# Expert stage of a 256-token transformer kernel: exact one-hot scatter into X, a moved branch, a reordered router

## The reference

```
logits = t @ w_router                                  # t: 256 x 1024, w_router: 1024 x 8
top_vals, top_idx = lax.top_k(logits, 2)
top_w = softmax(top_vals)
gates = sum(one_hot(top_idx, 8) * top_w)               # 256 x 8, two entries a row
for e in range(8):
    out = out + gates[:, e] * (silu(t @ w_gate[e]) * (t @ w_up[e])) @ w_down[e]
x = x + g2 * out                                       # g2: one row of 1024 of the modulation
return rmsnorm(x, final_norm)                          # then the second block
```

## Time and profile before

| | us |
|---|---|
| three runs | 2864.95, 2864.95, 2858.27 (median 2864.95) |
| the profiled execution | 2863.4 |
| its span from first to last instruction | 2861.5 |

### The profile page before, as it was taken

One profiled execution on the slowest core, in us unless ns is written; L12 is line 12 of the kernel. 1 busy time (PEld: TensorE's weight loads), 2 busy tenths in 40 slices (PEclk: granted clock), 3 DMA queues, 4 the chain that ended last, 5 costly groups with the idle time before them and its releaser, 6 DMA issues.

```text
span 2861.5 us, 38958 instructions
## 1 busy us (share of the span) xinstructions
PE 2668.1 (93%) x15384; PEld 2311.5 (81%) x15384; DVE 1982.5 (69%) x2853; ACT 1550.9 (54%) x2238; POOL 29.1 (1%) x40
## 2 busy tenths in 40 slices
PE   7688998978999999999996998998999999998998
PEld 3677988856888888888885997887898998787898
DVE  4768878886798899889896556555555556555555
ACT  2443444553777778777774444464444444364444
POOL 0000000020000000000000000000000000000000
PEclk9789998989999999999998999999999999999999
DMA  8537974614799999999995664433565664433563
GB/s 279 188 96 283 343 273 123 193 40 130 274 368 341 335 355 355 332 336 368 339 356 167 190 187 154 126 96 111 178 184 167 193 183 145 155 96 110 162 185 118
DMA packets 349599, 616.34 MB, mean 215 GB/s; under 512 B 20705, under 2 KB 174881, under 8 KB 349409
## 3 DMA queue, kind: packets, MB, share of 16 engines
q1 hardware_dynamic: 346402, 603.35, 63.1%
q0 software_dynamic: 1872, 5.99, 0.7%
q10 hardware_dynamic: 1136, 4.44, 0.4%
HBM read 612.66 MB, written 1.05 MB: 214 GB/s over the span
## 4 chain that ended last, share of the span: by engine, by line
PE 80%; DVE 11%; ACT 5%; DMA 2%; issue 2%; SPq 0%; DVEq 0%; ACTq 0%
PE pb L286 23%; PE pb L288 23%; PE pb L287 23%; PE pb L292 8%; DVE parts L260 3%; PE pb L408 2%; ACT parts L245 2%; DVE mod L1657 1%; DMA raw<-in_w_in 1%; PE pb L2609 1%; PE pb L2154 1%; DVE raw L625 1%; DMA raw<-in_ffn_w_up 0%; DMA X<-in_x 0%; DVE hTl L421 0%
## 5 line engine op out<-in xcount | busy, mean ns | idle before, releaser
L260 DVE TENSOR_TENSOR parts<-raw,parts 128x1024 fp32r<-128x1024 f32 (+2 forms) x1051 | 1263.7, 1216 | 614.9 <-ACT parts L245 580.4
L245 ACT ACTIVATE parts<-raw 128x1024 fp32r<-128x1024 f32 (+2 forms) x1051 | 1101.6, 1054 | 832.4 <-PE pb L288 693.9
L286 PE MATMUL pb<-parts,arenar 128*128 128x512 f32 (+2 forms) x1696 | 667.1, 393 | 12.6 <-DVE arenar L421 6.0
L287 PE MATMUL pb<-parts,arenar 128*128 128x512 f32 (+2 forms) x1696 | 649.9, 383 | 0.0
L288 PE MATMUL pb<-parts,arenar 128*128 128x512 f32 (+2 forms) x1696 | 649.5, 383 | 0.0
L286 PE MATMUL pb<-hTh,parts 128*128 128x256 f32 x1952 | 558.2, 286 | 6.0 <-DVE hTl L421 3.5
L287 PE MATMUL pb<-hTl,parts 128*128 128x256 f32 x1952 | 557.0, 285 | 0.0
L288 PE MATMUL pb<-hTh,parts 128*128 128x256 f32 x1952 | 556.8, 285 | 0.0
L286 PEld LDWEIGHTS pb<-hTh,parts 128*128 128x128 f32 x1952 | 379.7, 195 | 9.8 <-issue 5.2
L286 PEld LDWEIGHTS pb<-parts,arenar 128*128 128x128 f32 x1696 | 321.7, 190 | 76.9 <-issue 16.4
L287 PEld LDWEIGHTS pb<-hTl,parts 128*128 128x128 f32 x1952 | 379.7, 195 | 1.8
(11 more groups left out here) (286 smaller groups left out, 1996.5 us busy)
## 6 DMA issues: line engine op xcount, KB each, us to landing
raw<-in_moe_w_gate SPq DMA_DIRECT2D x176, 512.0 KB, 5.2
raw<-in_moe_w_up SPq DMA_DIRECT2D x176, 512.0 KB, 5.2
raw<-in_moe_w_down SPq DMA_DIRECT2D x176, 512.0 KB, 5.2
raw<-in_ffn_wg SPq DMA_DIRECT2D x88, 512.0 KB, 4.1
raw<-in_ffn_wu SPq DMA_DIRECT2D x88, 512.0 KB, 3.8
raw<-in_ffn_wd SPq DMA_DIRECT2D x88, 512.0 KB, 4.4
raw<-in_ada_wT SPq DMA_DIRECT2D x80, 512.0 KB, 5.2
raw<-in_w_in SPq DMA_DIRECT2D x72, 512.0 KB, 3.7
```

Source lines behind the costliest of these rows:

```text
L245: a.e.activation(self.part(t, 0), self.slot(t), ACT.Copy).then_inc(*a.up(self.c.hi, t.m))
L260: v.e.tensor_tensor(self.part(t, 1), self.slot(t), self.part(t, 0).bitcast(F32), ALU.subtract).then_inc(*v.up(self.c.lo, t.m))
L286: e.matmul(o, a[0], b[0], start=start, stop=False, skip_group_check=True)
L287: e.matmul(o, a[0], b[1], start=False, stop=False, skip_group_check=True)
```

## The change

- `Pm` is turned itself (not `Pm` times the gate) and stored for single-pass matmuls, which are exact for zeros and ones. The gate of each place is formed as a column `gcol` by two more matmuls of one column in `gates_pe`.
- The result of an expert is scaled by `gcol` and by the row of the modulation on DVE, straight from PSUM (`result_dve`, two instructions of 512 columns). ACT makes its high part `yh` (`result_act`), DVE its low part `yl` (`result_parts_dve`), and each scatter is two single-pass matmuls. Its result is added straight to X. `acc`, its memset and `add_dve` are gone.
- The scatters stand after tiles 2, 4, 6 of step (e+1, 2) and tile 0 of step (e+1, 3); gathers and gates of the next expert move by a tile or two. Expert 7's scatters use four banks.
- The flag is loaded at step 6 of the loop; the branch stands before expert 7's result and scatters.
- The router forms the logits token-major, per half of the tokens, without copy and transposes, PE's part for the first half standing ahead of the transposes of the second. The modulation's row is formed after the counting. An Exp is run early, so that its table is loaded. Expert 0's second gather has a bank of its own.

```diff
+    def result_dve(self, v, e):
+        K, c = self.K, self.c
+        v.wait_ge(*c.pe.val(("down", e)))
+        v.wait_ge(*c.bk[4].out.val(("PmT", e)))
+        if e:
+            v.wait_ge(*c.dv.val(("yl", e - 1, 1)))
+        for h in range(2):
+            b, cs = self.y_bank(h), slice(h * 512, (h + 1) * 512)
+            v.e.scalar_tensor_tensor(out=self.y[:, cs], in0=b.t[:, :], scalar=self.gcol[:, e % 2:e % 2 + 1],
+                                     in1=K.mod[:, 2, cs], op0=ALU.mult, op1=ALU.mult).then_inc(*v.up(b.out, ("y", e, h)))
+    def result_act(self, a, e):
...
+        for h in range(2):
+            cs = slice(h * 512, (h + 1) * 512)
+            a.wait_ge(*self.y_bank(h).out.val(("y", e, h)))
+            a.e.activation(self.ysb[0][:, cs], self.y[:, cs], ACT.Copy).then_inc(*a.up(c.ac, ("yh", e, h)))
+    def result_parts_dve(self, v, e):
...
+            v.wait_ge(*c.ac.val(("yh", e, h)))
+            v.e.tensor_tensor(self.ysb[1][:, cs], self.y[:, cs], self.ysb[0][:, cs].bitcast(F32),
+                              ALU.subtract).then_inc(*v.up(c.dv, ("yl", e, h)))
     def scatter_pe(self, t, e, tt, h):
-        c, b = self.c, self.c.bk[7]
-        t.wait_ge(*c.bk[6].out.val(("y", e, 1)))
-        t.wait_ge(*c.bk[5].out.val(("y", e, 0)))
...
-        mm1(t.e, b.t[:, :], self.PgT[:, e % 2, tt * P:(tt + 1) * P],
-            self.ysb[:, h * 512:(h + 1) * 512]).then_inc(*t.up(c.pe, ("scatter", e, tt, h)))
+        t.wait_ge(*c.dv.val(("yl", e, h)))
...
+        for i in range(2):
+            m = mm1(t.e, b.t[:, :], self.PmT[:, e % 2, tt * P:(tt + 1) * P],
+                    self.ysb[i][:, h * 512:(h + 1) * 512], i == 0, i == 1)
+    SCATTER = [(2, 2), (2, 4), (2, 6), (3, 0)]
+    GATHER = [(3, 2), (3, 4)]
+    GATES = (3, 6)
     def gates_pe(self, t, e):
...
+        for tt in range(2):
+            m = mm1(t.e, b.t[:, S:S + 1], self.Pm[:, e % 2, tt, :], gate[:, tt * 8 + e:tt * 8 + e + 1], tt == 0, tt == 1)
     def up_dve(self, v, i):
...
             self.step_dve(v)
+            if e and (j, q) == (2, 0):
+                self.result_parts_dve(v, e - 1)
     def pe(self, t):
-        self.K.enter_pe(t, "m2")
+        self.K.stats_pe("m2")
+        for tt in range(2):
+            self.K.xT_pe(t, "m2", tt)
+            self.logits_pe(t, tt)
         self.router_pe(t)
-        self.main.pe(t)
-        self.more(t, self.extra.pe)
+        self.main.pe(t, self.keep)
+        self.more(t, self.flags[t], self.extra_pe)
+        self.main.end_pe(t)
```

More of the change, by code:

```diff
@@ L559, in enter_act, with enter_dve @@
         self.W.hi(a, 2)
-    def enter_dve(self, v, st, add, norm, by_rows=False):
+    def enter_dve(self, v, st, add, norm, by_rows=False, early=1):
+        early = 0 if by_rows else early
         add(v, 0)
@@ L567, in enter_dve @@
         self.xT_dve(v, st, 0, 0)
-        if not by_rows:
-            self.W.low(v)
+        self.W.low(v, early)
         norm(v, 1)
@@ L572, in enter_dve @@
             self.xT_dve(v, st, tt, h)
-        self.W.low(v, 4 if by_rows else 3)
+        self.W.low(v, 4 - early)
     def hT_lhs(self, k, tt):
@@ L2091, in up_pe @@
             b = c.bk[self.up_bank(i, w)]
-            t.wait_ge(*c.bk[7].out.val(("gather", e, 4)))
+            for g0 in (0, 4):
+                if g0 < k0 + kg:
+                    t.wait_ge(*c.bk[self.gather_bank(e, g0)].out.val(("gather", e, g0)))
             if k0 == 0:
@@ L2191, in down_act, with pe @@
             self.step_act(a)
-        if j < 5:
-            return
-        a.wait_ge(*c.pe.val(("down", e)))
-        if e:
-            a.wait_ge(*c.pe.val(("scatter", e - 1, 1, 1)))
-        for h in range(2):
-            b = c.bk[5 + h]
-            a.e.activation(self.ysb[:, h * 512:(h + 1) * 512], b.t[:, :], ACT.Copy).then_inc(*a.up(b.out, ("y", e, h)))
+        if j == 5 and e < 7:
+            self.result_act(a, e)
     def down_dve(self, v, i):
-        for f in range(GROUPS[self.steps[i][1]][1] // P):
+        e, j = self.steps[i]
+        for f in range(GROUPS[j][1] // P):
             self.step_dve(v)
-    def pe(self, t):
+        if j == 5 and e < 7:
+            self.result_dve(v, e)
+    def pe(self, t, meanwhile=lambda t: None):
         n = len(self.steps)
@@ L2292, in router_pe @@
         mm1(t.e, b.t[:, 16:24], K.C["ones"], mask[:, 8:16], False, True).then_inc(*t.up(c.pe, "places"))
+        K.rows_pe(t, 1, 1, 2, (2, 3))
     def router_act(self, a):
         K, c = self.K, self.K.c
-        b = c.bk[0]
-        a.wait_ge(*c.pe.val("logits"))
-        a.e.activation(self.lgT, b.t[0:8, 0:S], ACT.Copy).then_inc(*a.up(b.out, "logits"))
+        a.wait_ge(*a.tail)
+        a.e.activation(K.warm, K.warm, ACT.Exp).then_inc(*a.up(c.ac))
+        a.wait_ge(*c.dv.val("top_gap"))
+        w1 = two(self.w12)[:, :, 1:2]
+        a.e.activation(w1, w1, ACT.Exp).then_inc(*a.up(c.ac, "top_exp"))
         for h in range(2):
@@ L3234, in mid_dve @@
     def mid_dve(self, v):
-        for tt in range(2):
-            self.moe.add_dve(v, tt)
         for tt in range(2):
```

201 lines of the change are left out of this document (116 added, 85 removed).

## The result

The changed kernel takes **2887.51 us** (four runs, 2886.51 to 2888.35), the kernel before 2863.40 (four, 2858.27 to 2864.95): ratio 1.0087, 95% interval 1.0070 to 1.0105. It is slower, as forecast, and inside the range, but 24 us slower where the sum said 15. The profiled execution spans 2885.9 us against 2861.5, 24.4 more.

What follows compares the result with a forecast made beforehand. PE (TensorE) was taken to bound the expert loop, DVE and ACT chains the stretches outside it. Seams +27.7, flag +1.0, end -11.4 and entry -2.6 gave +14.7 on 2863.4, so 2878 us; range 2860 to 2895.

Steps and rivals of the forecast that it cites:

- Scatter: Expert loop: single-pass scatters save 0.42 to 0.43 us each, four an expert, 1.7 us for each of seven experts.
- Chain: Each seam between experts: PE waits for `yl` at the first scatter, 3.5 us lost, bounds 3.0 and 4.3.
- Clock: After each seam's wait: PE drops to 1.2 GHz for eight matmuls, 1.6 us lost a seam, lower bound 0.
- low end of 2869: Whole kernel: the forecast time in us with all bounds low; all high gave 2897.
- Gates: Expert loop: two float32 matmuls of one column cost 0.45 us an expert, bounds 0.2 and 0.7.
- Seam: Each of seven seams between experts: net loss of 3.95 us from scatter, gates, waits and clock, 27.7 us in all.
- Flag: Mid-loop load of the flag on PE: costs 1.0 us, between 0 and 2.8.
- End: After the last down matmul: the norm starts earlier, gain 11.4 us, bound 6; the branch is hidden.
- Entry: Router to expert 0's first weight tile: gain 2.6 us, bounds a gain of 4 and a loss of 1.
- the hidden chain: Seams: `yl` is ready when PE reaches the first scatter, so the change is faster, 2842 us; chance 0.18.
- The rival of the end: After the last expert: less branch cover and slower chains lose half of the 11.4 us gain, 2884 to 2889; chance 0.08.

Runs made afterwards that it cites:

- e8: Changed kernel with scatters later and three groups apart, the DVE/ACT exchange over y taken apart, gate column at (4,3): 2843.4 us, 0.9945 of the kernel before.
- e9: Changed kernel with 30 useless float32 transposes of the identity on PE ahead of each first scatter of experts 0 to 6: 2868.6 us.
- e4: Changed kernel with the flag loaded where the branch stands, not in mid-loop, on PE, ACT and DVE: 2891.7 us.
- e3: Changed kernel with each expert's scatters, gathers and gate column two weight groups later: 2863.9 us.
- e7: Changed kernel with the last expert's four scatters through the one bank 7 again, not four banks: 2900.7 us.
- e10: Changed kernel with the branch behind the last expert's scatters again, flag still loaded in mid-loop: 2890.4 us.
- e1: Changed kernel with each expert's scatters, gathers and gate column three weight groups later: 2869.8 us, 1.0033 of the kernel before.
- e2: Changed kernel with each expert's scatters, gathers and gate column one weight group later: 2879.5 us.

## Why the prediction was right in direction and short in size

- **Scatter**: right. A scatter is 0.47 (953.98 to 954.45), against 0.87 for the float32 one (1.33 in the earlier trace rows less two slots of 0.2275): 0.40 saved, 0.42 said. e8 shows this gain undisturbed: C is 8.0 below before, where the sum without wait and clock gives 7 x (-1.7 + 0.45 + 0.1) = -8.05. The 0.1 in it, for waits at the later scatters, did not come; the 0.2 under Gates stands in its place.
- **Chain**: right by its links and nearly by its length. From DVE's free moment (943.25) to the scatter are 4.92 us, 4.6 said; PE stood 3.86 (944.31 to 948.17), 3.5 taken and 3.6 worked out: +0.3 a seam. The two scaled results take 1.40, not 1.20.
- **Clock**: the mechanism was right (e9), the term was mis-sized, and this is the step that failed most. I took the eight matmuls behind one gap of the earlier trace rows. Here 10 or 11 stand 0.427 apart: from 949.19 to 953.75 are 11 slots in 4.56 us, 2.5 at full clock, +2.06; and the scatter pair itself, which I had left out, takes 1.02 instead of 0.45, +0.57. Together 2.6 and not 1.6, which is what e9 gave back at this seam. The sum's low end of 2869 keeps the 1.6; with the bound of 0 that the term was given it would be 2858.
- **Gates**: 0.43 within expert 0 (0.45 said), but gates and gathers together 0.65 at six of the seams (1.11 less the fourth scatter's 0.46). What the other 0.2 is, no run isolates.
- **Seam**: 4.9 to 5.6, on average 5.34, against 3.95. Seven make 9.7; with the 0.43 of expert 0's gates and less the flag's 1.0 that did not come, they are the 9 us by which C exceeds the sum (37.75 against 28.7).
- **Flag**: 0, not 1.0 (the interval around it, and e4). By the Trainium skill (TensorE: Matmul & The Clock Gate, "Architectural detail") the queue of 64 would cover it; the trace agrees with the outcome (the interval around it is 0.00 longer than before). That the queue is the reason no run here shows.
- **End**: -9.7 instead of -11.4. The first result starts at +0.96 behind the last down matmul and not at +0.5, and the scatters took 0.9 us a pair (eight matmuls in 3.65) at a granted clock of 0.54 (1551.0 to 1554.6), so that the norm came at +7.44 and not at +5.7. I had counted the clock at the seams and forgotten it here, and taken the branch for hidden: it reached past the last matmul by 0.5. The chain itself was right: in e3, where neither shows, the norm starts at +5.85 and D is 11.25 less than before.
- **Entry**: -1.8 instead of -2.6. The gathers stood back to back in 3.86 us, as forecast, but began 26.05 us behind the end of A, where the forecast's 717 stands 25.2 behind it.
- **What no sum could hold**: A and E, -1.9 together here, but up to 12 us between two of the twelve profiles.
- **The rivals**: the hidden chain (2842) did not happen, but e8's 2843.4 is its time. It decides at the point the rival named, the moment at which `yl` is there when PE asks. What it missed is that asking later is not enough: the addition behind the scatter and the gate column ahead of a transpose each had to be given room as well. The rival of the end named 2884 to 2889, and 2887.5 lies in it, but by luck: the end missed 1.7 us and not half of its 11.4, and the rest came from the seams.

## What to carry to other kernels

A new chain across two engines is cheap where its consumer is asked late enough and each engine has other work between its links; moving the consumer alone uncovers the next wait, since an engine that was late had been catching up while the other stood. Cost the clock behind every long wait of PE (27 of 28 of 3.4 us and more lost it here), on the waited-for instructions too. And compare two profiles by stretches between marks that both programs have: e7 and after, 13 us apart, held 4.7 us that belong to the edit and what follows it.

## What the runs showed of the hardware that was not expected

- Of 28 waits of PE of 3.4 us and more in the loop (after, e4, e7 and e10) 27 were followed by 7 to 11 matmuls 0.427 us apart, one (e10, 3.44 us at 1273.53) by none. Of 21 waits of 2.1 to 2.4 us (e1, e2, e3) 8 were, by 2 to 8 matmuls, and 13 not; of the shorter ones alone none. The same program shows both at different seams, which may be a part of e1's spread of 2863 to 2878 us, though only one of its runs has a trace.
- 3.44 us of float32 transposes of the identity in the gap keep PE at the 2.4 GHz level (granted clock 1.00).
- The branch past the second pass takes a different time from one traced execution to the next. In the nine kernels that have it ahead of the last results and the load in mid-loop, DVE is idle 3.06 (e3) to 4.76 us (e2) before the first result, which starts 0.43 to 2.12 us behind the start of the last down matmul; without the branch it is 3.06 and 0.43 (e10). Only what reaches past that matmul is seen; what the branch itself waits for no row shows.
